# Three probability buffers, token-major filler and thinner selection rounds in the attention stages of a two-block transformer kernel

## What is computed

```python
# first block, twice ("a"): 8 query heads, 2 key heads of 64; window of 128; a sink in the softmax
aq, ak, av, rq, rk, rv, rg, ga, gb = jnp.split(rmsnorm(x, g_mix) @ w_in, SPLIT_POINTS, axis=-1)
ya = sliding_window_sink_attention(rope(aq), rope(ak), av, sinks) @ w_a
r = chunkwise_retention(rotate(rq), rotate(rk), rv)          # 4 heads, 128 x 256
yb = (normalised(r) * silu(rg)) @ w_b
x = x + (sigmoid(ga) * ya + sigmoid(gb) * yb) @ w_out
# second block, twice ("b"): 8 heads; each query sees the 128 keys that an indexer scores highest
top_val, top_idx = lax.top_k(score, 128)
ya = attention(q, k[top_idx], v[top_idx]) @ p_attn
o = gla_chunked(gq, gk, gv, log_sigmoid(g_lr @ w_gate + b) / 16)
yb = (layer_normalised(o) * silu(g_r)) @ p_gla
x = layer_norm(alpha * x + (sigmoid(gate_a) * ya + sigmoid(gate_b) * yb) @ w_out + b_out)
```

## Time and profile before

| what | value |
|---|---|
| runs | 3529.4, 3533.8, 3533.93 us; median 3533.8 |
| profiled execution | 3532.38 us, span 3530.60 us |
| mean granted clock of the tensor engine | 0.991 |
| busy: PE, PE weight loads, VectorE, ScalarE, POOL | 3416.4, 2781.8, 1513.3, 1415.4, 1443.5 us |
| DMA | 298.52 MB, 85 GB/s |
| the four attention stages | 69 to 186, 863 to 979, 1747 to 1840, 2702 to 2796 us |

### The profile page before, as it was taken

One profiled execution on the slowest core, in us unless ns is written; L12 is line 12 of the kernel. 1 busy time (PEld: TensorE's weight loads), 2 busy tenths in 40 slices (PEclk: granted clock), 3 DMA queues, 4 the chain that ended last, 5 costly groups with the idle time before them and its releaser, 6 DMA issues.

```text
span 3530.6 us, 45773 instructions
## 1 busy us (share of the span) xinstructions
PE 3416.4 (97%) x16650; PEld 2781.8 (79%) x16650; DVE 1513.3 (43%) x2471; ACT 1415.4 (40%) x2052; POOL 1443.5 (41%) x1100
## 2 busy tenths in 40 slices
PE   8999999999999999999999999999999999999998
PEld 6788878887688878887768887787777688877786
DVE  5524232226524432227851444434488414344435
ACT  4735332224734332223462444333344534353333
POOL 4334444444334544444423343444343233434442
PEclk9999999999999999999999999999999999999999
DMA  4122222222122222222211122222222111222221
GB/s 144 65 79 72 96 96 95 95 96 97 69 75 82 100 94 95 96 98 82 84 48 72 72 87 72 96 95 95 83 73 72 60 72 66 102 72 84 94 95 60
DMA packets 43814, 298.52 MB, mean 85 GB/s; under 512 B 4816, under 2 KB 5456, under 8 KB 8592
## 3 DMA queue, kind: packets, MB, share of 16 engines
q1 hardware_dynamic: 41696, 291.52, 22.9%
q10 hardware_dynamic: 1968, 4.94, 0.4%
HBM read 294.34 MB, written 2.10 MB: 84 GB/s over the span
## 4 chain that ended last, share of the span: by engine, by line
issue 53%; POOL 32%; PE 13%; DVE 1%; ACT 1%; POOLq 0%; DMA 0%; DVEq 0%; ACTq 0%; SPq 0%
POOL w_lo L338 31%; PE ps L457 4%; PE ps L459 4%; PE ps L458 4%; POOL own_lo L338 1%; POOLq L344 0%; DMA w_raw<-stream 0%; DVE arena L1723 0%; PE ps L541 0%; ACT arena L1180 0%; DVE x L1759 0%; POOLq L337 0%; DVE arena L1747 0%; ACT y_hi L1199 0%; ACT x L1518 0%
## 5 line engine op out<-in xcount | busy, mean ns | idle before, releaser
L338 POOL TENSOR_TENSOR w_lo<-w_raw,w_hi 128x512 fp32r<-128x512 f32 x1064 | 1400.4, 1348 | 2044.3 <-ACT w_hi L996 2044.3
L457 PE MATMUL ps<-x_hi,w_hi 128*128 128x512 f32 x2624 | 1043.7, 398 | 9.9 <-DVE x_lo L1538 6.1
L459 PE MATMUL ps<-x_hi,w_lo 128*128 128x512 f32 x2624 | 1024.9, 391 | 0.0
L458 PE MATMUL ps<-x_lo,w_hi 128*128 128x512 f32 x2624 | 1024.5, 390 | 0.0
L996 ACT ACTIVATE w_hi<-w_raw 128x1024 fp32r<-128x1024 f32 x532 | 531.5, 1048 | 458.6 <-PE ps L459 458.2
L457 PEld LDWEIGHTS ps<-x_hi,w_hi 128*128 128x128 f32 x2624 | 494.1, 188 | 148.6 <-issue 37.5
L459 PEld LDWEIGHTS ps<-x_hi,w_lo 128*128 128x128 f32 x2624 | 494.2, 188 | 105.6
L458 PEld LDWEIGHTS ps<-x_lo,w_hi 128*128 128x128 f32 x2624 | 494.7, 189 | 100.7 <-issue 2.4
L457 PE MATMUL ps<-y_hi,w_hi 128*128 128x512 f32 x1248 | 490.1, 393 | 17.7 <-DVE x L1759 13.0
L458 PE MATMUL ps<-y_lo,w_hi 128*128 128x512 f32 x1248 | 486.8, 390 | 0.0
L459 PE MATMUL ps<-y_hi,w_lo 128*128 128x512 f32 x1248 | 486.7, 390 | 0.0
(11 more groups left out here) (197 smaller groups left out, 3209.8 us busy)
## 6 DMA issues: line engine op xcount, KB each, us to landing
w_raw<-stream SPq DMA_DIRECT2D x274, 1024.0 KB, 4.8
x<-x_t SPq DMA_DIRECT2D x4, 512.0 KB, 6.0
rotary<-rot ACTq DMA_DIRECT2D x4, 512.0 KB, 3.6
y_t<-x SPq DMA_DIRECT2D x8, 256.0 KB, 2.1
ct<-consts ACTq DMA_DIRECT2D x2, 770.0 KB, 5.5
arena<-pos ACTq DMA_DIRECT2D x2, 256.0 KB, 4.0
vec<-vectors ACTq DMA_DIRECT2D x4, 116.0 KB, 2.1
ct<-consts ACTq DMA_DIRECT2D x1, 128.0 KB, 3.8
```

The lines of the kernel that those rows point to most:

```text
L338: ins = nc.gpsimd.tensor_tensor(low(c)[:, o:o + S], RAW[:, c % 2, o:o + S], high(c)[:, o:o + S].bitcast(F32), ALU.subtract)
L457: pe.matmul(ps, wh, xh, start=(k == 0), stop=False)
L458: pe.matmul(ps, wh, xl, start=False, stop=False)
L459: return pe.matmul(ps, wl, xh, start=False, stop=last)
```

## The change

- In the stream, the token-major panel of the first rv (a) and the first of gk (b) stand in front of the panels of `wa`.
- `tok_tiles` can give way after each group of 128 tokens (`halves`), and this panel is the last of the attention stage's filler: four pieces more, 32 in a and 20 in b. `pieces` becomes [2] * 14 + [1] * 3 and [2] + [1] * 16. What is left runs behind `outputs(15)`.
- `probs` has three buffers; the third is a free part of the scratch array. The indexer's dots keep two, under the name `dots_kept`.
- PE makes `scores(2)` before the loop and then `scores(i + 3)` behind the filler of pair i, in place of `scores(i + 2)` before it.
- VectorE takes the maxima of pairs 0 and 1 first, then per pair: rounds or rotation, `normalise(i)`, `maxima(i + 2)`. ScalarE takes `exponentials(i + 2)` in iteration i.
- The last 16 selection rounds are spread 2, 1, 2, 1, 2, 1, 2, 1, 2, 2 over ten pairs.
- The first rv goes to a place of its own (`values_a`), and the splits (`hi`) are moved to fit the new order.

The diff, without its changes of indices and names and with empty lines left out:

```diff
--- before.py
+++ after.py
@@ -76,9 +76,9 @@
-        out += _cols(wa, 512)
-        for h in range(RET_HEADS):
+        out += [rvp[0]] + _cols(wa, 512) + [rgp[0]]
+        for h in range(1, RET_HEADS):
...
@@ -93,7 +93,8 @@
-        out += _cols(gq) + _cols(i["p_attn_2"][l], 512) + _cols(gk)
+        gkp = _cols(gk)
+        out += _cols(gq) + [gkp[0]] + _cols(i["p_attn_2"][l], 512) + [gkp[1]]
...
@@ -394,8 +395,12 @@
                                 o=AR[:, 8 + j, b * P:(b + 1) * P]))
             return out
+        def dots_kept(i, nk):
+            return TMP[:, 2 * (i % 2):2 * (i % 2) + 2, 0:nk]
         def probs(i, nk):
-            return TMP[:, 2 * (i % 2):2 * (i % 2) + 2, 0:nk]
+            return YSCR[:, KD + 2:KD + 4, 0:nk] if i % 3 == 2 else TMP[:, 2 * (i % 3):2 * (i % 3) + 2, 0:nk]
         def probs_t(i, nk):
             a = 4 + 2 * (i % 2)
...
@@ -403,7 +408,11 @@
         def pieces(t):
-            return [2] * 11 + [1] * 6 if t == "a" else [1] * 16 + [0]
+            return [2] * 14 + [1] * 3 if t == "a" else [2] + [1] * 16
+        def rounds(i):
+            return (2, 1, 2, 1, 2, 1, 2, 1, 2, 2)[i] if i < 10 else 0
         def tiles_in(t, i):
...
@@ -416,6 +425,10 @@
+        def values_a(h):
+            return AR[:, 14 + 2 * (h % 2):16 + 2 * (h % 2), :] if h else YSCR[:, KD + 4:KD + 6, :]
...
@@ -527,6 +540,7 @@
                         bank_reader[b] = ("read",) + name(t // 2)
                         if t == NB - 1:
                             marks[("panel", n)] = marks[name(1)]
+                    if t % 2 or halves:
                         yield
             def tok_pair(n, name, ready, t, l):
...
@@ -604,13 +618,14 @@
                 scores(0)
                 scores(1)
                 run(fillers, pieces(t)[0])
+                scores(2)
                 for i in range(16):
                     transposes(i)
                     if i:
                         outputs(i - 1)
-                    if i + 2 < 16:
-                        scores(i + 2)
                     run(fillers, pieces(t)[i + 1])
+                    if i + 3 < 16:
+                        scores(i + 3)
                 outputs(15)
                 for _ in fillers:
                     pass
...
@@ -762,13 +777,13 @@
                         yield from retention_tiles(p, True)
                     for p in range(4):
                         yield from gemm_tiles(w["ga"] + p, KD, 2, XH, XL, h_ready, lambda m: (t, l, "ga", 2 * p + m), True)
+                    yield from tok_tiles(w["rv0"], h_ready, lambda m: (t, l, "rv", 0, m), True)
                 attention(pairs_a(l), l, t, fillers())
                 for p in range(2):
                     (gemm if p else gemm_first)(w["wa"] + p, 4, 4, YH, YL, lambda k: (t, l, "ao_lo", k),
                                                 lambda m: (t, l, "wa", 4 * p + m))
-                gemm_tok(w["rv"], h_ready, lambda m: (t, l, "rv", 0, m))
                 ring[0] = 2
                 gates = gate_tiles(l, w, t)
...
@@ -879,6 +894,7 @@
                         yield from gemm_tiles(w["ga"] + p, KD, 2, XH, XL, h_ready, lambda m: (t, l, "ga", 2 * p + m), True)
                     for p in range(2):
                         yield from gemm_tiles(w["gq"] + p, KD, 2, XH, XL, h_ready, lambda m: (t, l, "gq", 2 * p + m), True)
+                    yield from tok_tiles(w["gk"], h_ready, lambda m: (t, l, "gk", 0, m), True)
                 attention(pairs_b(l), l, t, fillers())
                 T.after((t, l, "glr"), ("w_gate", l), own=False)
...
@@ -889,8 +905,7 @@
-                for p in range(2):
-                    gemm_tok(w["gk"] + p, h_ready, lambda m: (t, l, "gk", p, m))
+                gemm_tok(w["wa"] + 2, h_ready, lambda m: (t, l, "gk", 1, m))
...
@@ -1053,14 +1068,15 @@
                     A.done(act.activation(pairs[i]["o"], PS[:, 2, 0:P], ACT.Copy), t, l, "o_read", i)
                 exponentials(0)
+                exponentials(1)
                 run(fillers, tiles_in(t, -1))
                 for i in range(17):
                     if i < 16:
                         read_transposes(i)
                     if i:
                         read_outputs(i - 1)
-                    if i < 15:
-                        exponentials(i + 1)
+                    if i < 14:
+                        exponentials(i + 2)
                     if i < 16:
                         run(fillers, tiles_in(t, i))
                     if i > 12:
...
@@ -1283,7 +1299,12 @@
+                            if (p, m) == (3, 1):
+                                hi(w["wa"])
+                    for m in range(2):
+                        read((t, l, "rv", 0, m), values_a(0)[:, m, :])
+                        yield
...
@@ -1292,13 +1313,12 @@
-                for p in range(2):
-                    hi(w["wa"] + p + 1)
+                hi(w["wa"] + 1)
-                        read((t, l, "rv", h, m), AR[:, 14 + 2 * (h % 2) + m, :], ACT.Copy, (t, l, "ao_lo", 3),
+                        read((t, l, "rv", h, m), values_a(h)[:, m, :], ACT.Copy, (t, l, "ao_lo", 3),
...
@@ -1315,8 +1335,7 @@
-                for _ in rv_reads(0):
-                    pass
+                hi(w["rv"] + 1)
...
@@ -1419,22 +1436,28 @@
+                            if (p, m) == (1, 1):
+                                hi(w["wa"])
+                    for m in range(2):
+                        tok_read("gk", 0, m)
+                        yield
+                hi(w["wa"] + 1)
-                hi(w["wa"] + 1)
-                hi(w["wa"] + 2)
-                for _ in tok_reads(w["gk"], "gk"):
-                    pass
+                for p in range(1, 3):
+                    hi(w["wa"] + p + 1)
+                for m in range(2):
+                    tok_read("gk", 1, m)
...
@@ -1601,11 +1624,11 @@
                         j = k - 1
                         lo(XL[:, j, :], dst(j), XH[:, j, :], [hi_name(j)], lo_name(j), own=False)
-            def attention(pairs, l, t, steps, per_pair):
+            def attention(pairs, l, t, steps):
                 def maxima(i):
                     U, c, nk = pairs[i], 8 * (i % 2), pairs[i]["nk"]
                     pr = probs(i, nk)
-                    V.after((t, l, "s", i), (t, l, "pt", i - 2) if i >= 2 else None, (t, l, "mask", i // 4))
+                    V.after((t, l, "s", i), (t, l, "pt", i - 3) if i >= 3 else None, (t, l, "mask", i // 4))
                     for v in range(2):
                         least = ST[:, 16 + U["sink"] + v:17 + U["sink"] + v] if U["sink"] is not None else -TAKEN
                         V.done(dve.tensor_tensor_reduce(pr[:, v, :], U["mask"], PS[:, 4 + v, 0:nk], -(HD ** -0.5), least,
...
@@ -1628,11 +1651,13 @@
                     V.done(dve.tensor_tensor(pr, pr, ST[:, c:c + 2].unsqueeze(2).broadcast_to([P, 2, nk]), ALU.mult),
                            t, l, "p", i)
+                maxima(0)
+                maxima(1)
                 for i in range(16):
-                    maxima(i)
-                    if t == "b" or i:
-                        run(steps, per_pair)
+                    run(steps, rounds(i) if t == "b" else min(i, 1))
                     normalise(i)
+                    if i + 2 < 16:
+                        maxima(i + 2)
                 for j in range(4):
                     lo(YL[:, j, :], AR[:, 14 + j, :] if t == "a" else AR[:, 8 + j, :], YH[:, j, :],
                        [(t, l, "ao_hi", j)], (t, l, "ao_lo", j))
...
```

38 lines of the change are left out of this document (18 added, 20 removed).

## The result

The changed kernel takes 3507.26 us (median of four runs, 3505.45 to 3509.82) against 3532.95 us for the kernel before on the same chip: a ratio of 0.9929, with a 95% interval of 0.9916 to 0.9943. The profiled execution took 3508.12 us, its span is 3506.3 us, 24.3 us shorter than the span before. The forecast was 3509.4 us, 24.4 us less than before. A part of the spread between runs is the clock's: the mean granted clock of the four runs is 0.993 in the shortest and 0.991 in the longest.

The account below looks back on a forecast made before the run. The tensor engine, busy 97% of the span, bounds the kernel. Idle time gone 22.2 us, less 1.2 seams and 1.7 slowed products, plus 5.1 clock, is 24.4: 3533.8 to 3509.4 us, range 3501 to 3520.

Parts of the forecast that it names:

- Idle time: Waits of the tensor engine in the four attention stages: 33.1 us before, 10.9 left, 22.2 gone.
- slowed products: VectorE's normalising products slowed beside POOL by 0.83 us; one taken in each b-stage, 1.7 us together.
- 5.7 against 7.3: none: In an a-stage VectorE's 5.7 us a pair, rotation included, fits PE's 7.3 us, so no wait.
- Seams: Cutting the contiguous token-major panel adds four seams of about 0.1 us on PE: 0.3 a stage, 1.2 in all.
- Clock: Clock falls behind the a-stages go with their idle time, 5.1 us back; the third, 3.4 us, stays.
- The rule of the window: VectorE's work for one pair must fit between two transposes, spare time not carried over; 3.3 us left a b-stage.
- The two pieces at pairs 11 to 13: In an a-stage two filler pieces make PE's period there 7.3 us instead of 4.7.
- 1 (rounds hidden): Selection rounds in the b-stages are hidden after all and the third clock fall goes: 3498 to 3506 us; chance 0.12.
- 2: Clock not given back behind the a-stages, or VectorE slowed more often: 3515 to 3519 us; chance 0.16.
- 3: Waits only move: b-stages keep theirs, a-stages keep 5 us for `wa`'s panel behind POOL: 3530 us; chance 0.07.
- 4: ScalarE's lag isn't absorbed; PE waits 2.7 us at 12 places: 32 us, 3541 us; chance 0.05.
- the forecast's 4 us lost in each four pairs: ScalarE in b-stages: at 2.66 us a table switch four pairs need some 21.5 us, losing about 4 us.

Follow-up runs that it names:

- filler_only: Changed kernel with two probability buffers and the old orders of scores, maxima, exponentials and rounds; the token-major filler stays: 3522.4 us.
- norm_first_early: Changed kernel with VectorE's order maxima(i+1), normalise(i), rounds, and the scores of pair i+2 ahead of the filler: 3497.8 us.
- old_rounds: Changed kernel with the selection rounds put back to two for each of pairs 0 to 7: 3507.7 us.
- norm_first: Changed kernel with VectorE's order alone turned to maxima(i+1), normalise(i), then rounds or rotation: 3497.6 us.
- buffers_only: Kernel before with three buffers, the new orders and rounds over ten pairs; token-major panel left where it was: 3510.0 us.
- half_rounds: Changed kernel with each of the last 16 selection rounds cut in two and the halves handed out over eleven pairs: 3499.5 us.
- act_extra: Changed kernel with ScalarE making each read of the transposed probabilities twice: 3509.5 us.

## Why the prediction was right, and where it was not

**The sum.** Its terms inside the stages held nearly; that the total came out within 0.1 us is luck.
- *Idle time.* Left were to be 10.9 and 1.7 for slowed products, 12.6; measured 12.7. By pairs of a b-stage (forecast, then first and second b-stage): pair 2 0.35, 0.33 and 0.19; pair 4 0.90, 1.06 and 1.06; pair 6 0.25, 0.08 and 0.07; pair 8 0.79, 1.33 and 1.33; pair 9 1.05, 0.82 and 0.81. At pair 8 a product of 768 columns took 1.69 where others take 0.96: most of the 0.85 a stage that was booked apart lies here. In front of `wa` 0.84 and 0.88 for 0.7.
- *Missed:* a wait of 0.80 in the first a-stage, at pair 1, and smaller ones of 0.14 and 0.16 at pair 4 of the two a-stages. The step that failed is "5.7 against 7.3: none". It took undisturbed durations, and two instructions of the rotation took 1.66 and 1.67 us beside POOL instead of 0.69. It also took PE's period of 256 keys, and pair 1, with 128, had 6.3 us and not 7.3 (from 863.73 to 870.00 in the second a-stage, where it did not wait).

```profile
79.72 1.66 DVE L1570 TENSOR_TENSOR arena<-arena,rotary 128x512 f32<-128x512 f32 x1
81.42 1.67 DVE L1572 TENSOR_TENSOR arena<-arena,scratch 128x512 f32<-128x512 f32 x1
```

```profile
84.06 0.44 PE L604 MATMUL ps<-ct,tmp 128*128 128x128 f32 x2 [0.80 <-DVE tmp L1651]
```

- *Seams.* Booked 0.3 a stage. PE's busy time at full clock grew by 1.3 and 1.4 in the a-stages (118.00 against 108.58 + 11.5 - 3.4) and fell by 0.4 and 0.3 in the b-stages: 2.0 for 1.2. The term was about the wrong thing. The panel's four pieces cost nothing: in filler_only, where the scores stand as before, the a-stages have 115.8 and 115.9 us at full clock against 116.7 and 116.6. It is the scores, which now stand behind each filler, that cost 0.13 us a pair (norm_first_early). Why the b-stages fell is open.
- *Clock.* The 5.1 us behind the a-stages came back as forecast, the last fall stayed as forecast, a new one of 1.7 behind the first b-stage did not stand in the sum.
- These give 20.4 - 2.0 + 5.1 - 1.7 = 21.8 of 24.3 us. Of the other 2.5, 1.7 are one clock fall less outside the stages (20.5 us before, 18.8 after, with PE at work), which nothing in the sum foresaw, and 0.8 over the remaining 3,070 us are not accounted for. These 2.5 us make up for what the seams and the new fall took.

**The rule of the window** was right for the changed kernel: the waits sit where the sums said, at even pairs and pair 9, they moved with the rounds in old_rounds, and spare time isn't carried over. It was put as a property of three buffers. norm_first shows that it is a property of the rounds standing ahead of a product that is due at once.

**Which part brings what** was the weakest. The two pieces at pairs 11 to 13 were to be what ends the long waits of the a-stages (7.3 against 4.7); buffers_only has single pieces there and waits 0.33. My expectations for the parts put 19 us on the filler, and 12 were measured; for the buffers 17, and 24 were measured. The total hid it, as the parts overlap.

**Rivals.** 1 (rounds hidden) is what half_rounds and norm_first make true: 3499.5 us, at the lower end of the 3498 to 3506 that it was given, and 3497.6, just below. 2 did not come, though one small fall of its kind did. 3 fell: nothing waits for POOL's half of `wa`'s second panel. 4 fell: no odd pair below 9 waits in a b-stage of the changed kernel, and act_extra costs 3 us in its stages. A table load takes 1.28 us in the changed kernel too, with the next activation 0.01 behind (129.38 and 130.67). The Trainium skill (ScalarE: Activation LUTs, What ACT_TABLE_LOAD costs) has 2.66 us a switch, and the trace does not agree. By that figure the nine loads of the first b-stage would take 12.4 us more, an estimate. act_extra gave ScalarE 11.3 us more there and the stage grew by 0.9, so the forecast's 4 us lost in each four pairs would hardly have come by that price either.

**Open.** What makes the clock fall behind the b-stages. In the changed kernel it fell at 1832.3, just behind the gate's matmuls with 32 rows of weights, which ran for 3.70 us from 1828.00. But old_rounds ran the same ones and lost nothing. With PE busy throughout, old_rounds kept its clock and norm_first, with fewer waits, lost it. Windows behind the first b-stage, at the gate's products, of old_rounds and of norm_first:

```profile
1830.00:1835.00 5.00, 5.00 (x20) 3.48 (x19) 0.00 (x0) 4.71 (x10) 4.14 (x4) 1.00 0.01 3
```

```profile
1825.00:1830.00 5.00, 5.00 (x15) 3.71 (x15) 0.00 (x0) 4.80 (x8) 3.37 (x3) 0.66 0.21 29
```

Since runs of one kernel differ in their clock too, one profiled execution of each can't say whether the kernels differ here. Differences of up to 5 us between two medians may therefore have a reason that the experiments didn't isolate.

## What to carry to other kernels

On an engine that works in order, put what has a deadline straight behind what releases it, and work that only has to be done some time behind that; before another buffer is added, see whether the order alone does it (here 6.5 us better with two buffers than the change with three). Where two engines hand pairs back and forth, the place of the producer's step and the consumer's order are one decision: move one of them alone and it may cost 44 us. Parts of a change that take away the same idle time don't add up, so test each alone.
